# The first norm's scale and shift: sums on VectorE while weights land, columns from 16 narrow products, transposed slabs scaled

## The reference, cut to what matters

```python
cond = jax.nn.silu(c)
mod = cond @ ada_w[layer] + ada_b[layer]          # 1024 x 6144 weights
sh1, sc1, g1, sh2, sc2, g2 = [m[:, None, :] for m in jnp.split(mod, 6, axis=-1)]
h = rms_norm(x, norm_mix[layer]) * (1 + sc1) + sh1
mix = mix_gla_gdn(h, ab_w_in, ...)                # begins with h @ ab_w_in, 1024 x 3608
x = x + g1 * mix
```

## Time and profile before

| what | value |
|---|---|
| runs | 1433.38, 1434.76, 1433.61 us; median 1433.61 us |
| the profiled execution's own time | 1438.11 us |
| its span, first to last instruction | 1436.0 us |
| busy in the span | PE 1251.2 us (87%), DVE 1076.3 (75%), ACT 690.6 (48%), POOL 311.4 (22%) |
| mean granted PE clock | 0.923 of full speed |

### The profile page before, as it was taken

How to read it: one execution, slowest core, us unless ns; L and a number is a source line. 1 busy time by engine, 2 the same in 40 slices (tenths; PEclk the granted TensorE clock), 3 DMA queues, 4 the chain that set the end, 5 groups by cost and what they waited for, 6 DMA issues and landing times. The chain is left out here.

```text
span 1436.0 us, 16425 instructions
## 1 busy us (share of the span) xinstructions
PE 1251.2 (87%) x6464; PEld 938.7 (65%) x6464; DVE 1076.3 (75%) x1282; ACT 690.6 (48%) x906; POOL 311.4 (22%) x133
## 2 busy tenths in 40 slices
PE   4799997768899779999999859967996899999992
PEld 1477786548754658888888744435445688888882
DVE  2757986675845749999999847867256599999994
ACT  2221434233432227777777622238222577777770
POOL 2100000010000014555554200000000165555431
PEclk9799999789999679999999969989996899999996
DMA  9778635224230649999999283453016599999944
GB/s 330 268 250 288 217 110 179 72 85 160 110 118 30 264 159 357 391 378 373 385 368 377 79 307 118 147 215 121 0 50 257 209 375 386 368 385 384 377 182 191
DMA packets 63859, 338.19 MB, mean 236 GB/s; under 512 B 11837, under 2 KB 12350, under 8 KB 49700
## 3 DMA queue, kind: packets, MB, share of 16 engines
q1 hardware_dynamic: 51428, 311.00, 58.2%
q0 software_dynamic: 11536, 22.91, 4.6%
q10 hardware_dynamic: 816, 3.20, 0.6%
HBM read 325.60 MB, written 28.84 MB: 247 GB/s over the span
## 5 line engine op out<-in xcount | busy, mean ns | idle before, releaser
L1445 PE MATMUL ps<-ring_r,work_r 128*128 128x512 f32 x536 | 212.8, 397 | 0.0
L2485 DVE TENSOR_TENSOR ring_r<-ring,early_mod_r 128x2048 fp32r<-128x2048 f32 x76 | 188.8, 2514 | 23.8 <-ACT early_mod_r L1601 23.4
L1443 PE MATMUL ps<-early_mod_r,work_r 128*128 128x512 f32 x468 | 188.4, 402 | 8.1 <-DVE work_r L2788 4.7
L1601 ACT ACTIVATE work<-ps 128x512 f32<-128x512 f32 (+3 forms) x121 | 80.6, 671 | 226.5 <-PE ps L1445 134.4
L1444 PE MATMUL ps<-early_mod_r,work_r 128*128 128x512 f32 x468 | 183.8, 393 | 0.0
L842 POOL TENSOR_TENSOR work<-work,early_mod 128x1024 f32<-128x1024 f32 x30 | 148.4, 4945 | 158.9 <-ACT work L1601 158.9
L1601 ACT ACTIVATE work_r<-ring 128x2048 fp32r<-128x2048 f32 (+2 forms) x87 | 133.8, 1558 | 88.8 <-PE ps L956 88.8
L1601 ACT ACTIVATE early_mod_r<-ring 128x2048 fp32r<-128x2048 f32 x79 | 147.6, 1910 | 0.4 <-PE ps L1445 0.3
L1443 PE MATMUL ps<-work_r 128*128 128x512 f32 x324 | 133.1, 411 | 7.7 <-DVE work_r L2788 4.7
L947 PE MATMUL ps<-const,work 128*128 128x128 f32 (+1 forms) x696 | 103.6, 291 | 38.1 <-DMA work<-h_rows,row_i 12.0
L2485 DVE TENSOR_TENSOR ring_r<-ring,work_r 128x2048 fp32r<-128x2048 f32 x52 | 132.8, 2578 | 4.5 <-ACT work_r L1601 4.5
(11 more groups left out here) (324 smaller groups left out, 2330.7 us busy)
## 6 DMA issues: line engine op xcount, KB each, us to landing
ring<-in_moe_w_up_dram SPq DMA_DIRECT2D x33, 2048.0 KB, 10.4
early_mod<-in_ada_w_dram SPq DMA_DIRECT2D x80, 512.0 KB, 4.5
ring<-in_moe_w_gate_dram SPq DMA_DIRECT2D x19, 2048.0 KB, 9.6
hT<-in_moe_w_down_dram SPq DMA_DIRECT2D x16, 2048.0 KB, 9.8
ring<-in_moe_w_down_dram SPq DMA_DIRECT2D x15, 2048.0 KB, 10.0
work<-in_moe_w_gate_dram SPq DMA_DIRECT2D x14, 2048.0 KB, 10.3
ring<-in_ab_w_in_dram SPq DMA_DIRECT2D x7, 2048.0 KB, 10.4
ring<-in_ada_w_dram SPq DMA_DIRECT2D x4, 2048.0 KB, 23.5
```

What stands on the lines that cost most here:

```text
L1443: mm(out, a_lo, w_hi, start=first_, stop=False)
L1445: return mm(out, a_hi, w_lo, start=False, stop=last_)
L1601: return nc.scalar.activation(out, in_, fn, **kw)
L2485: v.tensor_tensor(half_of(l, m, half, True), half_of(l, m, half), highs[(2 * m + half) % MHIGHS].bitcast(F32), ALU.subtract).then_inc(SV.s ...
```

## The change

1. The 2048 columns are loaded as eight row slabs `k` of 128 rows (1 MiB each, 8 KB of one row per partition) instead of four column blocks (2 KB pieces). `x` moves from ACT's queue to the second place in SP's, ahead of the slabs. ACT loads only the identity and ones (256 columns) at the start; the other constants (424 and 1472 columns) are issued after ACT's part of the norm. `c`, the bias and the gain come as columns in one load of 32 columns.
2. DVE alone sums all eight slabs, as each lands, into one 128x2048 tile; the last slab in two halves.
3. PE makes columns of the sum with eight products of one column for each half, on top of the bias (a small product with the identity), and DVE forms `shift_col0` and `scale_col0`.
4. `x` is only normalised by ACT, transposed by PE and copied by ACT to `xnT`. Scale and shift are then applied on the transposed slabs: ACT makes `hT_high`, DVE makes the full value and `hT_low`, slab by slab.
5. The projection's first quarter waits for its own two slabs, no longer for the whole of `h`.
6. POOL's small parameter loads wait for chunk 0 of `ab_w_in` instead of the first block of `ada_w`; the gain's 512 KB broadcast and POOL's shift additions are gone. The ring slots come free from DVE's sums instead of PE's.

```diff
-            sp.dma_start(cond, a["c_cols"]).then_inc(cond_in, 16)
-            load_columns(("ada", 0), a["ada_w"][0], [512 * n for n in FIRST])
+            sp.dma_start(first_cols, a["c_cols"]).then_inc(cond_in, 16)
+            sp.dma_start(x[:], a["x"][0].rearrange("(t p) d -> p t d", p=P)).then_inc(x_in, 16)
+            for k in range(KD):
+                landed = chunk_in[k // 2] if k % 2 else first_in[k // 2]
+                sp.dma_start(first_rows[k], a["ada_w"][0].rearrange("(k p) f -> p k f", p=P)[:, k, 0:2 * D]).then_inc(landed, 16)
...
-                    sp.wait_ge(FIRST_PE.sem, FIRST_PE.at(0, f"m{c - RING}"))
+                    sp.wait_ge(FIRST_DVE.sem, FIRST_DVE.at(0, ("k1", "k3", "k5", "k7b")[c - RING]))
...
-            pool.wait_ge(chunk_in[0], 16)
-            nc.gpsimd.dma_start(gain1, bc(a["norm_mix"][0])).then_inc(gains_in[0], 16)
+            nc.gpsimd.memset(side_pad, 0.0).then_inc(pad_ready, 1)
+            pool.wait_ge(chunk_in[0], 32)
...
+            def first_columns(half):
+                out = bank(4 + half, 2, KD // 2)
+                mm(out, ident, first_bias.rearrange("p (s k) -> p s k", s=2)[:, :, 4 * half:4 * half + 4], start=True, stop=False, skip_group_check=True)
+                pe.wait_ge(FIRST_DVE.sem, FIRST_DVE.at(0, "k7" + "ab"[half]))
+                for k in range(4):
+                    for s_ in range(2):
+                        ins = mm(out[:, s_, k:k + 1], first_halves[:, s_, half, cols(k)], cst("ones", 0, 1), start=False, stop=(k == 3 and s_ == 1),
+                                 skip_group_check=True)
...
             def project_ab():
-                pe.wait_ge(norm_act.sem, norm_act.at(0, "ev3"))
-                pe.wait_ge(norm_dve.sem, norm_dve.at(0, "ev3"))
...
+                            if n == 0 and t == 0:
+                                pe.wait_ge(norm_act.sem, norm_act.at(0, f"hi{2 * q + 1}"))
+                                pe.wait_ge(norm_dve.sem, norm_dve.at(0, f"lo{2 * q + 1}"))
...
+                for t in range(TT):
+                    f(x[:, t], x[:, t], ACT.Copy, scale=rstd[:, t:t + 1]).then_inc(norm_act.sem, norm_act.one(f"xn{t}"))
+                for t in range(TT):
+                    act.wait_ge(norm_pe.sem, norm_pe.at(0, f"turned{t}"))
+                    b = 4 + 2 * (t % 2)
+                    f(xnT[:, :, cols(t)], ps[:, b:b + 2].rearrange("p b (k n) -> p (b k) n", k=4)).then_inc(norm_act.sem, norm_act.one(f"ev{t}"))
...
+                    f(hT_high[:, k], xnT[:, k], ACT.Identity, bias=shift_col0[:, k:k + 1], scale=scale_col0[:, k:k + 1]
+                      ).then_inc(norm_act.sem, norm_act.one(f"hi{k}"))
...
+                for k in range(KD - 1):
+                    dve.wait_ge(chunk_in[k // 2] if k % 2 else first_in[k // 2], 16)
+                    if k == 0:
+                        v.tensor_scalar(first_sum, first_rows[0], cond[:, 0:1], None, ALU.mult).then_inc(S.sem, S.one("k0"))
+                    else:
+                        dve.wait_ge(S.sem, S.at(0, f"k{k - 1}"))
+                        v.scalar_tensor_tensor(out=first_sum, in0=first_rows[k], scalar=cond[:, k:k + 1], in1=first_sum,
+                                               op0=ALU.mult, op1=ALU.add).then_inc(S.sem, S.one(f"k{k}"))
+                    if k == 2:
+                        variance()
+                    elif k == 3:
+                        refine_rstd()
...
+                for k in range(KD):
...
+                        v.tensor_copy(shift_col0[:, c], col[:, 0]).then_inc(S.sem, S.one("shift" + half))
...
+                    v.tensor_scalar(hT_full[:, k], xnT[:, k], scale_col0[:, k:k + 1], shift_col0[:, k:k + 1], ALU.mult, ALU.add
+                                    ).then_inc(norm_dve.sem, norm_dve.one(f"full{k}"))
...
+                    v.tensor_tensor(hT_low[:, k], hT_full[:, k], hT_high[:, k].bitcast(F32), ALU.subtract).then_inc(norm_dve.sem, norm_dve.one(f"lo{k}"))
+                    if k in (1, 3):
+                        low_part(k // 2)
```

More of the change, by code:

```diff
@@ L184, in build_block @@
         ident = cst("ident")
[L187 removed]
+        first_cols = carve("par", 4 * KD)
+        cond, first_bias, first_gain = first_cols[:, 0:KD], first_cols[:, KD:3 * KD], first_cols[:, 3 * KD:4 * KD]
+        shift_col0, scale_col0 = (carve("par", KD) for _ in range(2))
         w2aug = carve("par", HEADS * GLA_DK)
@@ L210, in build_block @@
         early_in = sem("early_in")
+        ident_in = sem("ident_in")
+        first_in = [sem(f"first_in{s}") for s in range(RING)]
         cond_in = sem("cond_in")
@@ L246, in build_block @@
         cond_act = Steps(sem("cond_act"), ["exp"])
[L247 to L250, removed]
+        amod_dve = Steps(sem("amod_dve"), ["a20", "a21"])
+        norm_act = Steps(sem("norm_act"), ["ss0", "ss1", "ss2", "ss3", "root", "xn0", "xn1", "xn2", "xn3", "ev0", "ev1", "ev2", "ev3"] + [f"hi{k}" for k in range(KD)])
+        norm_dve = Steps(sem("norm_dve"), ["var", "n1", "n2", "n3", "rstd"] +
+                         [f"{n}{k}" for k in range(KD) for n in ("full", "lo")])
         TN_ACT = Steps(sem("tile_norm_act"), ["ss", "root"])
@@ L404, in build_block @@
         h = carve("work", TT, D)
[L406 to L409, removed]
+        xnT = work[:, 0:4096].rearrange("p (k n) -> p k n", k=KD)
+        first_sum = work[:, 4096:6144]
+        first_halves = first_sum.rearrange("p (s a f) -> p s a f", s=2, a=2)
+        gain2 = mod[:, 512:1536]
+        first_rows = [ring.rearrange("p s k f -> p (s k f)")[:, 2048 * k:2048 * k + 2048] for k in range(KD)]
         junk_wide = work[:, NWORK - D:NWORK]
@@ L956, in parts_mm @@
                 return mm(out, a[0], w[1], start=False, stop=stop)
[L958 to L969, removed]
+            def first_columns(half):
[6 more added lines that the diff above has]
+                                 skip_group_check=True)
+                ins.then_inc(FIRST_PE.sem, FIRST_PE.one("ab"[half]))
             def mod_sums(l, lo, hi):
@@ L992, in turn_rows_normed, with turn_first @@
                 ins.then_inc(RN_PE.sem, RN_PE.one("turned"))
[L994 to L1008, removed]
+            def turn_first(t):
+                pe.wait_ge(norm_act.sem, norm_act.at(0, f"xn{t}"))
+                if t >= 2:
+                    pe.wait_ge(norm_act.sem, norm_act.at(0, f"ev{t - 2}"))
+                for k in range(KD):
+                    ins = turn(bank(4 + 2 * (t % 2) + k // 4)[:, cols(k % 4)], x[:, t, cols(k)])
+                ins.then_inc(norm_pe.sem, norm_pe.one(f"turned{t}"))
             def project_ab():
-                pe.wait_ge(norm_act.sem, norm_act.at(0, "ev3"))
-                pe.wait_ge(norm_dve.sem, norm_dve.at(0, "ev3"))
                 def sums(ct):
@@ L1554, in experts @@
                                 over_block(j)
-            first_mod()
-            pe.wait_ge(const_in, 16)
-            norm()
+            pe.wait_ge(ident_in, 16)
+            pe.wait_ge(cond_in, 16)
+            for t in range(TT):
+                turn_first(t)
+            pe.wait_ge(norm_act.sem, norm_act.at(0, "ev2"))
+            for half in range(2):
+                first_columns(half)
             project_ab()
```

128 lines of the change are left out of this document (49 added, 79 removed).

## The result

The change is faster, by less than forecast: 1426.36 us (median of six runs, 1423.9 to 1429.23) against 1434.18 for the kernel before on the same chip (six runs, 1433.03 to 1438.94), ratio 0.995 [0.9934, 0.9966]. That is 7.8 us less, where 13.6 were forecast; 1420.0 us was the prediction, 1425.0 the upper end of its range. Its engines are busy much as before: PE 1232.5 us (87%), DVE 1066.1 (75%), ACT 700.7 (49%), POOL 327.7 (23%), mean clock 0.927.

What follows compares the result with a forecast made beforehand. Before 62 us DMA queue order decides, then TensorE bounds. First product 22.4 us earlier, less 0.9 before quarter 3, 5.0 before chunk 1, 2.6 to the clock and 0.3 rounding, leaves 13.6: 1420.0 us, range 1411.5 to 1425.

Steps and rivals of the forecast that it cites:

- rival B: Opening's loads: DMA flows at only 355 GB/s, side unit 0 lands at 62.0, 7.8 us remain, 1425.8 us; chance 0.12.
- Narrow products: TensorE, columns of the sum: eight one-column products take 3.5 us at half clock, ending at 35.3.
- First product: TensorE, start of the projection: first product at 40.0 us instead of 62.4, with 41.2 as the other bound.
- POOL's issues: POOL's parameter issues, now beside VectorE's scaling: one scaling took 1.07 instead of 0.48 before, so first product perhaps 41.2.
- unit 0: First side unit, last in SP's queue: lands at 56.2 us, and from there VectorE's order sets the pace.
- the stand before quarter 3: TensorE in chunk 0: waits for low_part(3), behind side units 0 and 1 on VectorE; 0.9 us given back.
- the stand before chunk 1: TensorE waits from 65.5 to 70.5 for VectorE's first bank copy: 5.0 us given back, plus 2.6 to the clock.
- I let this shift stand to the end: From chunk 2 on, loads, waits and units keep their places relative to TensorE, so the 13.6 us gain stays.
- The same 13.6 makes 1420.0 against the median: Whole kernel: 13.6 us off the profiled 1438.11 makes 1424.5, and off the median 1433.61 makes 1420.0.
- A: Side units in time: no dips, unit 0 near 50, TensorE never stands, chunk 2 at 72.0, 1411.5 us; chance 0.20.
- C: SP's queue between slabs and unit 0: small loads collide, dips of over 18.7 us, about 1437 us; chance 0.03.
- D: Given back later: the 48 side units, not TensorE, set the projection's end, no change at all; chance 0.03.

Runs made afterwards that it cites:

- repeats: The kernel before and the changed kernel, both run again unchanged on one chip: 1438.02 us and 1429.23 us.
- loads_cut: Changed kernel, loads of side units 0 to 7 ahead of chunks 2 and 3's weights, units 3 to 47 loading 64 of 1024 columns: 1389.56 us.
- units_later_before: Kernel before, with the eight side units of chunk 0 spread over chunks 2 to 7 on VectorE: 1440.06 us, ratio 1.0059.
- units_later: Changed kernel, with the eight side units of chunk 0 spread over chunks 2 to 7 on VectorE: 1420.05 us, ratio to before 0.9911.
- eight_first: Changed kernel, with the loads of side units 0 to 7 issued ahead of the weights of chunks 2 and 3: 1422.28 us, ratio to before 0.9899.

## Why the prediction failed, step by step

**The opening: right in mechanism, each term small.** The first half of the last slab's sum ran from 29.7 to 31.0, forecast 31.1. The slabs came at 420 GB/s over 16 us, so rival B, which went with 355, did not come. The Trainium skill, "DMA: Bandwidth & Descriptors", Specifications, has about 358 GB/s as the limit for one core; the row of 420 disagrees. Narrow products: forecast 3.5 us for eight, from a row at half clock; the first eight took 1.95 at clock 1.00, right after TensorE had turned the last two tiles. First product forecast 40.0, measured 37.43. POOL's issues did not slow VectorE's scaling (0.54 us, not 1.07). But unit 0 landed at 57.5 and 58.6 instead of 56.2. These 1.3 and 2.4 us, and the 2.6 and 2.3 by which the first product came early, all went into the stand before quarter 3: 5.1 and 5.8 instead of 0.9. After that stand the clock was at 0.50 too, which I had priced only before chunk 1; it made the stand before chunk 1 shorter (3.7 and 3.9 instead of 5.0) and cost nothing more, since chunk 1 waits for the bank copy. Chunk 1 started at 72.6 and 73.7 instead of 70.5, chunk 2 at 81.25 and 83.75 instead of 80.5. The gain at chunk 2 was 12.8 and 10.3 us, not 13.6.

**"I let this shift stand to the end": held to the first router product, open behind it.** At that product, the first of layer 0's choice of experts, TensorE is 12.6 us earlier, 493.19 to 480.61:

```profile
493.19 0.69 PE L1421 MATMUL ps<-work,const 128*128 128x64 f32 x2 [4.76 <-DVE work L2668]
```

```profile
480.61 0.69 PE L1409 MATMUL ps<-work,const 128*128 128x64 f32 x2 [4.75 <-DVE work L2659]
```

(before, then the change; in the repeats 497.10 and 484.41, 12.7). From there to the end of the span it takes 942.8, 940.4 and 936.5 us in the three profiles of the kernel before and its variant, and 939.9 to 944.5, mean 942.8, in the ten of the change and its variants, loads_cut apart. So up to 3 us may be given back over 940 us of experts and attention, where the edit changes no work (it only makes the two layers share a few semaphores). Three profiles with a spread of 6 us against ten with one of 4.6 do not show it, and no run tried a cause: it stays open.

**"The same 13.6 makes 1420.0 against the median": the step that failed.** The gain was worked out of one execution of before, which took 1438.11 us, and taken off a median 4.5 us lower. This is what became of the 13.6:

| gain, us | first pair of profiles | repeats |
|---|---|---|
| at chunk 2 | 12.8 | 10.3 |
| at the first router product | 12.6 | 12.7 |
| in the span | 11.8 | 9.9 |
| in the times of the two executions | 12.1 | 10.5 |
| between the medians | 7.8 | 8.8 |

Of the 5.8 us missed in the first pair, 4.3 lie in the last step alone. The profiled execution of before stands 3.9 us above the median of its six, that of the change 0.3 below the median of its six. So that 1424.5, the forecast for the profiled execution, came within 1.5 us of the 1426.02 measured is in part luck: it sets one of the longer executions of before against a middling one of the change. Against the 17 runs of the repeats' chip the medians differ by 7.65 us. Executions of before go down to 1430 on that chip and to 1426.5 on another. I had no row that says where those save their time, and let the range end at 1425.0 as if the gain did not depend on the execution. One profile hints at the place: units_later_before's was the lowest of its seven executions (1436.4 against a median of 1440.06), and it spent the 936.5 us above behind the router, 3.9 and 6.3 less than the two profiles of before, which were among the longest of theirs. One such profile shows no cause: why executions differ, and why the medians lie closer together than the profiles, stays open.

**The rivals.** A, the units in time, did not happen by itself; units_later and eight_first made it happen, and gave chunk 2 at 70.3 to 70.7 (72.0 in the forecast) but 1420 and 1422 us: from chunk 2 to the gate product they take 6.6 and 5.2 us more than the change, since the later loads then run short. B's 1425.8 us lies near the result, but its mechanism did not come, nor did C: the small loads made dips like those of before. D did not come in the projection (from chunk 2 to the gate product 148.6 and 152.0 us before, 149.8 and 151.0 in the change); whether something is given back behind the router stays open, as said.

## What to carry to other kernels

When an opening gets shorter, ask what stood behind it just in time: here eight background steps with loads at the end of a queue, ahead of a copy that the bound engine needs. Follow the last of such steps to the copy, not the first, and see whether a load can pass weights that are wanted 20 us later; that reordering gained nearly as much at chunk 2 (10.6 us) as moving the work to later chunks (11.0). A gain worked out of one execution belongs to that execution; against a median it needs a margin of the size of their scatter.

## What the runs showed of the hardware that I had not expected

- TensorE kept full clock over the first eight products of one column, right after two turned tiles (1.95 us, clock 1.00), where layer 1's sixteen after a wait of 5.70 us ran at 0.50. With the second eight the clock fell: 0.59 in 34 to 36 us, 0.50 in 36 to 40.
- Loads of 8 KB a partition moved 420 GB/s (12 to 28 us), those of 2 KB 387 to 408.
- Small loads cost wherever they are put: with POOL's parameters late, the dip moved with them (from 42 to 46 us to 55 to 60) and the time stayed. Busy by stretch of that run (clock, DMA share and GB/s last):

```profile
55.00:60.00 5.00, 5.00 (x23) 4.03 (x22) 2.88 (x4) 0.47 (x2) 3.83 (x8) 1.00 0.97 135
```
